# Building the expert router's row lists with a small matrix product instead of a scatter through memory

## The chip, the cores and the metric

The kernel runs on one core of a Trainium2 chip, as one launch. The metric is the device time of that launch in microseconds (us), the median of several executions. All arithmetic is float32.

## What is computed

The reference is a trunk of two layers (`DEPTH = 2`) over 512 latent tokens and 256 context tokens of width 1024. Each layer has a mixer part (a gated long convolution beside latent attention), which the change does not touch, and then a mixture of experts. The first layer handles all 768 tokens, the second only the 512 latent ones. The part that matters here:

```python
def hier_moe(u, w_rg, b_rg, w_re, b_re, w_gate, w_up, w_down):
    t = u.reshape(-1, D_MODEL)
    lg = (t @ w_rg)
    g_sel = jnp.argmax(lg + b_rg, axis=-1)                      # 1 of 8 groups
    p_g = take(softmax(lg), g_sel)
    le_g = (t @ w_re).reshape(T, 8, 8)[g_sel]; be_g = b_re[g_sel]
    _, local = lax.top_k(le_g + be_g, 2)                        # 2 of 8 experts in it
    w_local = softmax(take(le_g, local))
    expert = g_sel * 8 + local; weight = p_g * w_local
    # each expert e: y += weight * ((silu(x @ w_gate[e]) * (x @ w_up[e])) @ w_down[e])
```

There are 64 experts (`NE`), each with 3 MB of weights. Every token picks two of them.

## The kernel before

The program is a sequence of stages. `stage` (line 110 on) opens buffers and semaphores, runs one instruction list per engine, and ends with a barrier over all engines, so nothing of one stage starts before everything of the one before has ended, except transfers that were started early on purpose.

For each layer `experts` (line 2113 on) runs these stages:

1. `norm_stage` normalises the residual. While it runs, `first_round` on the SP queue starts to load the weights of the first four experts into a ring of four places (`RU = 4`; buffers `wgu`, 64 KB per partition, and `wd`, 32 KB per partition).
2. `router_stage` (line 1540 on). For each tile of 128 tokens (`NT` = 6 in the first layer, 4 in the second) TensorE transposes the tokens to rows and computes the 72 router scores (lines 1611 and 1616). The rows are written to the DRAM tensor `rows_in`, twice, once for each of the two picks (line 1583). VectorE then finds the group and the two experts of each token in a chain of small instructions, each waiting for the last (`Chain`, line 120). The result is a one-hot array `sel` (line 1699). Three products on TensorE (lines 1621 to 1623) count for each pick how many earlier picks went to the same expert: `rank`, and the totals `cnt`. `rank_done` announces them.
   After that VectorE computes for each pick the place `dest` in a table: the expert's column and the position in it, or, for an expert with more than 64 picks, a column of an overflow block (lines 1719 to 1742). GpSimd sends each pick's row number to that place in the DRAM tensor `slots` with one indirect DMA per tile and pick, 12 in the first layer and 8 in the second (line 1597). SP waits for all of them, loads the table back into `m.table` (line 1585) and ends the stage.
3. `moe_stage` (line 1788 on) goes through the 64 experts. For expert j GpSimd gathers up to 64 token rows from `rows_in` by the table's column j (line 1834, after a clearing `memset`, line 1830, for each of the first four), TensorE transposes them (1777), multiplies with gate and up weights (`gate_up`, 1761), ScalarE and VectorE form `h` (1911, 1928), TensorE multiplies with the down weights (`down_both`, 1769), and GpSimd scatters the result to `rows_out` by the same column (1841). SP loads expert j's weights when expert j-4's down product is done (lines 1784 and 1785), so the fifth expert's weights start only when the first expert has gone all the way through. The first four and the last four experts are unrolled, those between are a loop (`rounds`).
4. `overflow_stage` handles experts with more than 64 picks, `combine_stage` adds the weighted results to the residual.

The order of the work around the change is thus set by the barriers, by VectorE's chain, and in the experts' stage by the ring of four weights. The lines that decide when the next weights may be fetched:

```python
            def load(j, b, r):
                if inner(j) or j >= RU:
                    wait(sp, s["down_done"], j - (RU - 1))
                    load_expert(sp, a, l, j, wgu[:, b], wd[:, b], loaded[b])
```

Of the kernel before, what the change touches and what calls it, by code (L numbers as in the profile page):

```python
# [69 lines left out]
def layout_constants():  # L70
# [34 lines left out]
    iota = np.zeros((P, 96), f)  # L105
    iota[:, 0:64] = np.arange(64)
    iota[:, 64:88] = np.arange(24)
    iota[:, 88] = np.arange(P)
# [1433 lines left out]
def router_stage(nc, m, l, a, consts, streams, dram):  # L1542

# [6 lines left out]
    NOV = overflow_blocks(n_tok)  # L1550
    NB = NE + NOV
    QM = (n_tok - 1) // SLOTS
    R = NG + NE
    LOW = -3.0e38
    sems = ["consts_in", "wr_in", "bias_in", "tr_done", "lg_done", "tr_evac_a", "tr_evac_v", "lg_evac", "u_out0", "u_out1", "dve",
            "exps", "hot_done", "rank_done", "filled", "fill_out", "dest_done", "sc_out", "table_in"]
    bufs = [("wr", [P, KC, R]), ("bias", [P, R]), ("lg", [P, NT, R]), ("utok", [P, 2, D]), ("triu", [P, P]), ("iota", [P, 96]),
            ("gb", [P, NT, NG]), ("c", [P, NT, NG]), ("hot_g", [P, NT, NG]), ("e", [P, NT, NG]), ("leg", [P, NT, EG]),
            ("beg", [P, NT, EG]), ("val", [P, NT, EG]), ("hot1", [P, NT, EG]), ("hot2", [P, NT, EG]), ("big", [P, NT, NE]),
            ("sel", [P, 2, NT, NE]), ("both", [P, NT, NE]), ("before", [P, NT + 1, NE]), ("rank", [P, NT, NE]), ("cnt", [P, NE]), ("ovf", [P, NE]),  # L1560
            ("incl", [P, NE]), ("base", [P, NE]), ("one", [P, NE]), ("r", [P, 16, NT]), ("ex", [P, 2, NT]),
            ("q", [P, 2, NT]), ("pos", [P, 2, NT]), ("eid", [P, 2, NT]), ("ob", [P, 2, NT]), ("z", [P, 2, NT]), ("dest", [P, 2, NT]),
            ("dest_i", [P, 2, NT], I32), ("num", [P, 2, NT]), ("num_i", [P, 2, NT], I32), ("fill", [SLOTS, NB], I32),
            ("cmp", [P, NOV, NE]), ("oe", [P, NOV])]
    table = dram["table"][l]
    with stage(nc, f"route{l}", sems, bufs) as (block, s):
# [3 lines left out]
        def _(sp):  # L1570
# [5 lines left out]
            sp.dma_start(s["iota"][:], consts["iota"]).then_inc(s["consts_in"], 16)  # L1576
# [24 lines left out]

        @block.tensor
        def _(pe):
# [35 lines left out]
        def _(dve):  # L1639
            link = Chain(dve, s["dve"])  # L1640
            nc.vector.memset(s["before"][:, 0], 0.0)
            for j in range(NT):
                dve.wait_ge(s["tr_done"], j + 1)
                if j >= 2:
                    dve.wait_ge(u_out[j % 2], 32 * (j // 2))
# [13 lines left out]
            iota8 = over(s["iota"][:, None, 0:NG], NT, NG)  # L1659
# [25 lines left out]
            big4 = s["big"][:].rearrange("p t (g j) -> p t g j", g=NG)  # L1685
            for src, dst in ((s["lg"][:, :, NG:R].rearrange("p t (g j) -> p t g j", g=NG), s["leg"]),
                             (over(s["bias"][:, NG:R].rearrange("p (t g j) -> p t g j", t=1, g=NG), NT, NG, EG), s["beg"])):
                link(nc.vector.tensor_tensor(big4, src, hot_over, ALU.mult))
                link(nc.vector.tensor_reduce(dst[:], s["big"][:].rearrange("p t (g j) -> p t j g", g=NG), axis=AX.X, op=ALU.add))
# [4 lines left out]
            picked(s["ex"][:, 0], s["leg"][:], s["hot1"][:])  # L1694
            picked(s["ex"][:, 1], s["leg"][:], s["hot2"][:])
            link(nc.vector.tensor_tensor(row(6), s["ex"][:, 0], s["ex"][:, 1], ALU.max))
            nc.vector.tensor_tensor(s["ex"][:], s["ex"][:], over(row(6)[:, None, :], 2, NT), ALU.subtract).then_inc(s["exps"], 1)
            for k, hot in enumerate((s["hot1"], s["hot2"])):
                last = nc.vector.tensor_tensor(s["sel"][:, k].rearrange("p t (g j) -> p t g j", g=NG), hot_over,
                                               over(hot[:, :, None, :], NT, NG, EG), ALU.mult)  # L1700
            link(last)
            link(nc.vector.tensor_tensor(s["both"][:], s["sel"][:, 0], s["sel"][:, 1], ALU.add))
# [7 lines left out]

            dve.wait_ge(s["exps"], 4)
# [5 lines left out]

            dve.wait_ge(s["rank_done"], 1)
            nc.vector.tensor_copy(s["rank"][:], m.ps[:, 6, 0:NT * NE].rearrange("p (t e) -> p t e", e=NE))
            nc.vector.memset(s["one"][:], 1.0)  # L1720
            link(nc.vector.tensor_copy(s["cnt"][:], m.ps[:, 7, 0:NE]))
            link(nc.vector.tensor_scalar(s["ovf"][:], s["cnt"][:], float(SLOTS), None, ALU.is_gt))
            for q in range(2, QM + 1):
                link(nc.vector.scalar_tensor_tensor(s["ovf"][:], s["cnt"][:], float(q * SLOTS), s["ovf"][:], ALU.is_gt, ALU.add))
            link(nc.vector.tensor_tensor_scan(s["incl"][:], s["one"][:], s["ovf"][:], 0.0, ALU.mult, ALU.add))
            link(nc.vector.tensor_tensor(s["base"][:], s["incl"][:], s["ovf"][:], ALU.subtract))
            for k in range(2):
                for vals, out in ((s["rank"][:], s["pos"]), (over(s["iota"][:, None, 0:NE], NT, NE), s["eid"]), (over(s["base"][:, None, :], NT, NE), s["ob"])):
                    link(nc.vector.tensor_tensor(s["big"][:], s["sel"][:, k], vals, ALU.mult))
# [58 lines left out]
def moe_stage(nc, m, l, a, dram, ring):  # L1788
# [6 lines left out]
    with stage(nc, f"moe{l}", sems, bufs) as (block, s):  # L1795
# [384 lines left out]
```

## Time and profile before

| | us |
|---|---|
| median of 3 runs | 3326.81 (3319.71 to 3334.4) |
| profiled execution | 3327.05 |
| its span, first to last instruction | 3325.3 |
| PE busy | 2768.1 (83%) |
| DVE busy | 869.4 (26%) |
| ACT busy | 630.3 (19%) |
| POOL busy | 372.7 (11%) |

The engines are PE (TensorE; PEld is its weight load), DVE (VectorE), ACT (ScalarE), POOL (GpSimd) and SP (SyncE, which issues most transfers). "Busy" adds up the times of an engine's instructions. The span and the time of the same execution differ by 1.75 us. The mixers and the two expert parts follow each other, so a share of the whole span is a mean over stages that have different limits.

### The profile page before, as it was taken

What the parts mean: (1) busy time and instruction counts of PE and PEld (TensorE: products, weight loads), DVE (VectorE), ACT (ScalarE), POOL (GpSimd) and SP (SyncE); (2) the same over time, 40 slices, a digit from 0 to 9 for tenths busy, and PEclk for the clock granted to TensorE, in tenths of its full rate; (3) what the DMA queues carried; (4) which work ended last, traced back from release to release, by engine and by line L of the source; (5) the groups of instructions that cost most, each with busy time, mean ns of one, the idle gap of its engine ahead of it and who ended that gap; (6) DMA issues with size and microseconds to landing.
All of it is one profiled execution on the core that took longest, in us unless ns stands there. A gap on an engine that the chain in (4) does not pass through costs nothing. (4 is left out here: it accounts for less than half of the span.)

```text
span 3325.3 us, 36651 instructions
## 1 busy us (share of the span) xinstructions
PE 2768.1 (83%) x13443; PEld 1707.5 (51%) x13443; DVE 869.4 (26%) x1741; ACT 630.3 (19%) x1210; POOL 372.7 (11%) x444
## 2 busy tenths in 40 slices
PE   6998987999999982888888578799999749888884
PEld 3445656556655562555555355556544435555553
DVE  3442247144200014111111233424300131111113
ACT  2332210133200010211111121023200111111111
POOL 0000001000000001222222100100000022222221
PEclk7877998999999985999999779999999779999995
DMA  9553111001013032899999521201022429999982
GB/s 334 212 190 139 64 49 65 4 11 43 19 38 107 0 152 83 318 407 393 382 393 382 224 79 48 73 6 48 0 76 88 170 102 408 385 394 383 396 343 78
DMA packets 207096, 589.02 MB, mean 177 GB/s; under 512 B 48336, under 2 KB 105475, under 8 KB 156708
## 3 DMA queue, kind: packets, MB, share of 16 engines
q1 hardware_dynamic: 183428, 556.40, 43.9%
q0 software_dynamic: 23584, 31.53, 2.8%
q8 instruction: 49, 0.80, 0.1%
q14 instruction: 35, 0.29, 0.0%
HBM read 577.29 MB, written 56.68 MB: 191 GB/s over the span
## 5 line engine op out<-in xcount | busy, mean ns | idle before, releaser
L1761 PE MATMUL ps<-wgu,moe_xt 128*64 128x256 f32 x4096 | 509.1, 404 | 147.1 <-DMA wd<-in_w_down_e 144.6
L1761 PEld LDWEIGHTS ps<-wgu,moe_xt 128*64 128x64 f32 x4096 | 336.3, 145 | 277.9 <-issue 168.6
L1356 PE MATMUL ps<-u,w_merge 128*128 128x512 f32 (+1 forms) x768 | 282.3, 526 | 4.1 <-DVEq L1373 4.1
L1769 PE MATMUL ps<-wd,moe_ht 128*64 128x512 f32 x1024 | 247.8, 605 | 1.5 <-DVE moe_ht L1934 1.5
L720 PE MATMUL ps<-u,w_hy 128*128 128x512 f32 (+1 forms) x576 | 213.8, 530 | 18.4 <-PEq L123 18.4
L1928 DVE TENSOR_TENSOR moe_h<-ps,moe_sg 64x256 f32<-64x256 f32 x128 | 54.5, 426 | 664.0 <-ACT moe_sg L1911 664.0
L1356 PEld LDWEIGHTS ps<-u,w_merge 128*128 128x128 f32 x768 | 147.0, 192 | 135.0 <-issue 123.9
L1841 POOL DMA_INDIRECT rows_out<-moe_y,table x128 | 118.5, 926 | 800.7 <-DVE moe_y L1892 788.6
L1777 PE MATMUL ps<-ident,moe_xg 64*128 64x64 f32 x1024 | 140.2, 278 | 74.2 <-DMA moe_xg<-rows_in,table 74.2
L1777 PEld LDWEIGHTS ps<-ident,moe_xg 64*128 64x128 f32 x1024 | 122.7, 199 | 123.0 <-issue 123.0
L720 PEld LDWEIGHTS ps<-u,w_hy 128*128 128x128 f32 x576 | 109.9, 194 | 113.7 <-issue 109.2
L1911 ACT ACTIVATE moe_sg<-ps 64x256 f32<-64x256 f32 x128 | 48.0, 375 | 618.8 <-PE ps L1761 618.8
L1892 DVE COPY moe_y<-ps 64x512 f32<-64x512 f32 x128 | 88.7, 693 | 265.9 <-PE ps L1769 265.9
L1414 PE MATMUL ps<-mix,w_out 128*128 128x512 f32 (+1 forms) x384 | 141.0, 530 | 7.7 <-PEq L123 7.7
L1380 DVE TENSOR_TENSOR merge_t<-ps,merge_sig 128x1024 f32<-128x1024 f32 (+1 forms) x24 | 25.1, 1047 | 397.5 <-ACT merge_sig L1368 397.5
L1834 POOL DMA_INDIRECT moe_xg<-rows_in,table x128 | 120.0, 937 | 42.9 <-issue 36.6
L1414 PEld LDWEIGHTS ps<-mix,w_out 128*128 128x128 f32 x384 | 74.1, 194 | 74.6 <-issue 71.4
L1898 ACT ACTIVATE moe_y<-ps 64x512 f32<-64x512 f32 x128 | 75.6, 590 | 173.4 <-PE ps L1769 173.4
L1898 ACT ACTIVATE moe_xt<-ps 128x512 f32<-128x512 f32 x128 | 76.5, 598 | 166.5 <-PE ps L1777 166.5
L1769 PEld LDWEIGHTS ps<-wd,moe_ht 128*64 128x64 f32 x1024 | 62.3, 136 | 83.5 <-issue 73.1
L1187 PE MATMUL ps<-vt,attn_pt 128*128 x832 | 101.6, 271 | 0.6 <-DVE attn_pt L1288 0.5
L1187 PEld LDWEIGHTS ps<-vt,attn_pt 128*128 128x128 f32 x832 | 98.8, 192 | 1.1 <-ACT attn_pt L1246 1.1
(295 smaller groups left out, 3318.9 us busy)
## 6 DMA issues: line engine op xcount, KB each, us to landing
wgu<-in_w_gate_e SPq DMA_DIRECT2D x128, 1024.0 KB, 8.4
wgu<-in_w_up_e SPq DMA_DIRECT2D x128, 1024.0 KB, 11.0
wd<-in_w_down_e SPq DMA_DIRECT2D x128, 1024.0 KB, 17.2
prep_w<-in_w_ada SPq DMA_DIRECT2D x24, 2048.0 KB, 14.7
w_merge<-in_w_in SPq DMA_DIRECT2D x32, 512.0 KB, 4.7
w_hy<-in_w_in SPq DMA_DIRECT2D x6, 2048.0 KB, 8.4
transfer<-prep_out POOLq DMA_DIRECT2D x10, 1024.0 KB, 7.6
rows_in<-route_utok SPq DMA_DIRECT2D x20, 512.0 KB, 3.6
```

The source lines that it names most:

```text
L720: last = nc.tensor.matmul(m.ps[:, 2 * (i % 2) + t, 0:n], w[:, (i // HC) % 2, c, (i % HC) * P:(i % HC + 1) * P], m.u[:, c, at:at + n], star ...
L1187: last = nc.tensor.matmul(m.ps[:, 6 + u % 2, 0:VD], s["pt"][:, u % 2, k], m.vt[:, k0 // P + k, bass.ds((i * 2 + h) * VD, VD)], start=k == ...
L1356: last = nc.tensor.matmul(m.ps[:, bank, 0:n], w[:, b, w_at + c], z[:, c, at:at + n], start=c == 0, stop=c == kn - 1)
L1414: last = nc.tensor.matmul(m.ps[:, 2 * (k % 2) + t, 0:n], w[:, k // 4, c, (k % 4) * P:(k % 4 + 1) * P], m.mix[:, c, at:at + n], start=c == ...
L1761: last = nc.tensor.matmul(ps[k * SLOTS:(k + 1) * SLOTS, 0:DE], xt[:, c], wgu[:, k, c], start=c == 0, stop=c == KC - 1)
L1769: last = nc.tensor.matmul(ps[k * SLOTS:(k + 1) * SLOTS, 0:512], ht[:, c], wd[:, c, k * 512:(k + 1) * 512], start=c == 0, stop=c == 1)
L1777: last = nc.tensor.transpose(ps[:, c * SLOTS:(c + 1) * SLOTS], src.rearrange("p (q c) -> p c q", c=n)[:, c], ident[0:SLOTS, 0:SLOTS])
L1834: nc.gpsimd.indirect_dma_start(out=xg[:, j % 4], out_offset=None, in_=dram["u"], in_offset=bass.IndirectOffsetOnAxis(ap=m.table[0:SLOTS, j ...
L1841: nc.gpsimd.indirect_dma_start(out=dram["y"], out_offset=bass.IndirectOffsetOnAxis(ap=m.table[0:SLOTS, j:j + 1], axis=0), in_=y[:, j % 2], ...
L1892: copy(y[:, b % 2, half * 512:(half + 1) * 512], m.ps[half * SLOTS:(half + 1) * SLOTS, 5 + b % 2]).then_inc(sem, 1)
L1898: return nc.scalar.activation(out, in_, ACT.Copy)
L1928: nc.vector.tensor_tensor(h[:, b % 2], m.ps[SLOTS:2 * SLOTS, b % 2, 0:DE], sg[SLOTS:2 * SLOTS, b % 2], ALU.mult).then_inc(s["h_done"], 1)
```

## The change

The table is no longer sent through DRAM. In the router stage two one-hot arrays are made: `slot`, which marks for each pick its position among the 64 of its expert, and `tag`, which is `sel` times the pick's row number minus 1536. The product of the two over all picks, 12 (8) accumulating matrix products on TensorE, is the table, negative where a slot is filled and 0 where it is empty. VectorE adds 1536 and has `table` for the scatter. A second array `rows` folds both picks of a token to one row number, so that `rows_in` holds each token once and is written once. The weights of the picks are computed later in VectorE's chain than before.

The columns for overflow blocks, and the list of the experts they belong to, are made in the experts' stage: `late_slots` at the start of VectorE's list there, before its first `h`; a product on TensorE after the fourth expert; `late_lists` on VectorE after that. To hand `sel`, `pos`, `cnt` and `iota` over, they are kept in buffers of `experts`. `rows` is allocated ahead of the ring of weights.

```diff
+            iota[:, 88 + k * TT + j] = k * TOK + j * P + np.arange(P) - 2 * TOK
...
-def router_stage(nc, m, l, a, consts, streams, dram):
+def router_stage(nc, m, l, a, consts, streams, dram, picks):
...
-            sp.wait_ge(s["filled"], 1)
-            sp.dma_start(table.rearrange("(s b) o -> s (b o)", b=NB), s["fill"][:]).then_inc(s["fill_out"], 16)
             for j in range(NT):
...
-                for k in range(2):
-                    sp.dma_start(dram["u"][k * TOK + j * P:k * TOK + (j + 1) * P], s["utok"][:, j % 2]).then_inc(u_out[j % 2], 16)
-            sp.wait_ge(s["sc_out"], 16 * 2 * NT)
-            sp.dma_start(m.table[0:SLOTS, 0:NB], table.rearrange("(s b) o -> s (b o)", b=NB)).then_inc(s["table_in"], 16)
+                sp.dma_start(dram["u"][j * P:(j + 1) * P], s["utok"][:, j % 2]).then_inc(u_out[j % 2], 16)
             for k in range(2):
-                sp.wait_ge(u_out[k], 16 * NT)
-            sp.wait_ge(s["table_in"], 16)
-
-        @block.gpsimd
-        def _(pool):
-            nc.gpsimd.memset(s["fill"][:], NO_ROW).then_inc(s["filled"], 1)
-            pool.wait_ge(s["fill_out"], 16)
-            pool.wait_ge(s["dest_done"], 2)
-            for k in range(2):
-                for j in range(NT):
-                    nc.gpsimd.indirect_dma_start(out=table, out_offset=bass.IndirectOffsetOnAxis(ap=s["dest_i"][:, k, j:j + 1], axis=0),
-                                                 in_=s["num_i"][:, k, j:j + 1], in_offset=None,
-                                                 bounds_check=SLOTS * NB - 1, oob_is_err=False).then_inc(s["sc_out"], 16)
-            pool.wait_ge(s["sc_out"], 16 * 2 * NT)
+                sp.wait_ge(u_out[k], 16 * (NT // 2))
...
             last.then_inc(s["rank_done"], 1)
+            pe.wait_ge(s["slots_done"], 1)
+            for k in range(2):
+                for j in range(NT):
+                    last = nc.tensor.matmul(m.ps[0:SLOTS, 0, 0:NE], s["slot"][:, k, j], s["tag"][:, k, j],
+                                            start=k == 0 and j == 0, stop=k == 1 and j == NT - 1)
+            last.then_inc(s["table_done"], 1)
...
-            dve.wait_ge(s["exps"], 2)
-            link(nc.vector.tensor_reduce(row(2), s["e"][:], axis=AX.X, op=ALU.add))
-            picked(row(3), s["e"][:], s["hot_g"][:])
...
-            picked(s["ex"][:, 0], s["leg"][:], s["hot1"][:])
-            picked(s["ex"][:, 1], s["leg"][:], s["hot2"][:])
-            link(nc.vector.tensor_tensor(row(6), s["ex"][:, 0], s["ex"][:, 1], ALU.max))
-            nc.vector.tensor_tensor(s["ex"][:], s["ex"][:], over(row(6)[:, None, :], 2, NT), ALU.subtract).then_inc(s["exps"], 1)
...
             last.then_inc(s["hot_done"], 1)
 
+            rows = iota[:, 88:88 + 2 * TT].rearrange("p (k t) -> p k t", k=2)[:, :, 0:NT]
+            for k in range(2):
+                nc.vector.tensor_tensor(s["tag"][:, k], sel[:, k, 0:NT], over(rows[:, k, :, None], NT, NE), ALU.mult)
+            dve.wait_ge(s["exps"], 2)
+            link(nc.vector.tensor_reduce(row(2), s["e"][:], axis=AX.X, op=ALU.add))
+            picked(row(3), s["e"][:], s["hot_g"][:])
+
+            dve.wait_ge(s["rank_done"], 1)
+            link(nc.vector.tensor_copy(s["rank"][:], m.ps[:, 6, 0:NT * NE].rearrange("p (t e) -> p t e", e=NE)))
+            for k in range(2):
+                last = nc.vector.tensor_tensor(s["big"][:, k], sel[:, k, 0:NT], s["rank"][:], ALU.mult)
+            link(last)
+            link(nc.vector.tensor_reduce(pos[:, :, 0:NT], s["big"][:], axis=AX.X, op=ALU.add))
+            for k in range(2):
+                last = nc.vector.tensor_tensor(s["slot"][:, k], over(iota[:, None, 0:SLOTS], NT, SLOTS), over(pos[:, k, 0:NT, None], NT, SLOTS), ALU.is_equal)
+            last.then_inc(s["slots_done"], 1)
+            nc.vector.tensor_copy(cnt[:], m.ps[:, 7, 0:NE])
+            picked(s["ex"][:, 0], s["leg"][:], s["hot1"][:])
+            picked(s["ex"][:, 1], s["leg"][:], s["hot2"][:])
...
+            dve.wait_ge(s["table_done"], 1)
+            listed = m.ps[0:SLOTS, 0, 0:NE]
+            link(nc.vector.tensor_scalar(s["late"][:], listed, -float(TOK), -float(TOK), ALU.is_ge, ALU.mult))
+            nc.vector.scalar_tensor_tensor(m.rows[0:SLOTS, 0:NE], listed, float(NO_ROW), s["late"][:], ALU.add, ALU.add)
+            nc.vector.tensor_scalar_add(m.table[0:SLOTS, 0:NE], listed, float(NO_ROW))
...
@@ moe_stage
-                                             in_offset=bass.IndirectOffsetOnAxis(ap=m.table[0:SLOTS, j:j + 1], axis=0),
+                                             in_offset=bass.IndirectOffsetOnAxis(ap=m.rows[0:SLOTS, j:j + 1], axis=0),
...
+            def late_lists():
+                pe.wait_ge(s["late_slots"], 1)
+                for k in range(2):
+                    for j in range(NT):
+                        last = nc.tensor.matmul(m.ps[0:SLOTS, 7, 0:NOV], s["slot"][:, k, j], s["tag"][:, k, j],
+                                                start=k == 0 and j == 0, stop=k == 1 and j == NT - 1)
+                last.then_inc(s["late_table"], 1)
+
             x_transposes(0, 0, 0)
-            rounds(pe, body)
+            rounds(pe, body, late_lists)
...
+            late_slots()
+            rounds(dve, body, late_lists)
...
@@ experts
-    with ExitStack() as whole:
+    with nc.sbuf_tensor(f"rows{l}", [P, NE + overflow_blocks(TOK)], I32) as rows, ExitStack() as whole:
+        m.rows = rows
```

How the instructions move on VectorE, in the first layer's router stage, from the copy of the ranks on. Before, every row from here to the cast of `route_num_i` stands ahead of the first indirect scatter (the second pick repeats rows L1729 and L1730):

```order
L1719 COPY route_rank<-ps 128x384
L1720 MEMSET route_one 128x64
L1721 COPY route_cnt<-ps 128x64
L1722 TENSOR_SCALAR route_ovf<-route_cnt 128x64
L1724 SCALAR_TENSOR_TENSOR route_ovf<-route_cnt,route_ovf 128x64 x10
L1725 SCALAR_TENSOR_TENSOR route_incl<-route_one,route_ovf 128x64
L1726 TENSOR_TENSOR route_base<-route_incl,route_ovf 128x64
L1729 TENSOR_TENSOR route_big<-route_sel,route_rank 128x384
L1730 TENSOR_REDUCE route_pos<-route_big 128x6
...
L1734 SCALAR_TENSOR_TENSOR route_q<-route_pos,route_q 128x12 x10
```

Now (line numbers of the changed program), from the totals before it on; `route_slot` is the array that the table's product waits for:

```order
L1682 TENSOR_TENSOR route_before<-route_before,route_both 128x64 x5
L1689 TENSOR_TENSOR route_tag<-pick_sel,pick_iota 128x384 x2
L1691 TENSOR_REDUCE route_r<-route_e 128x6
L1654 TENSOR_TENSOR route_c<-route_e,route_hot_g 128x48
L1655 TENSOR_REDUCE route_r<-route_c 128x6
L1695 COPY route_rank<-ps 128x384
L1697 TENSOR_TENSOR route_big<-pick_sel,route_rank 128x384 x2
L1699 TENSOR_REDUCE pick_pos<-route_big 128x12
L1701 TENSOR_TENSOR route_slot<-pick_iota,pick_pos 128x384 x2
L1703 COPY pick_cnt<-ps 128x64
```

Four instruction groups (L1695 to L1701) are left between the ranks and the product; the overflow arithmetic has gone from here.

It stands now at the start of VectorE's list in the experts' stage, ahead of the first `moe_h` (some rows of the piece; the order before had `moe_h` as the stage's first row):

```order
L1923 MEMSET moe_one 128x64
L1924 TENSOR_SCALAR moe_ovf<-pick_cnt 128x64
...
L1930 TENSOR_TENSOR moe_big<-pick_sel,moe_base 128x384 x2
L1932 TENSOR_REDUCE moe_ob<-moe_big 128x12
...
L1943 TENSOR_TENSOR moe_slot<-pick_iota,moe_at 128x384
L1944 TENSOR_TENSOR moe_tag<-pick_iota,moe_ob 128x144
...
L1949 TENSOR_TENSOR moe_cmp<-moe_incl,pick_iota 128x1536
L1951 TENSOR_REDUCE moe_oe<-moe_cmp 128x24
L1952 TENSOR_SCALAR moe_oe<-moe_oe 128x24
L1953 CAST over<-moe_oe 128x24
L1954 CAST over<-moe_incl 128x1
L1909 TENSOR_TENSOR moe_h<-ps,moe_sg 64x256
```

The whole piece is 28 instructions in either layer, all but a few linked one to the next.

## Rows read from the trace of the kernel before

**Rows 1.** The page: the costliest group, and one of its transfers by its issues
```profile
L1761 PE MATMUL ps<-wgu,moe_xt 128*64 128x256 f32 x4096 | 509.1, 404 | 147.1 <-DMA wd<-in_w_down_e 144.6
...
wd<-in_w_down_e SPq DMA_DIRECT2D x128, 1024.0 KB, 17.2
```

**Rows 2.** Windows: stretch, its us, busy of each engine, clock, DMA share, GB/s
```profile
1346.00:1400.00 54.00, 50.28 (x354) 29.54 (x352) 9.98 (x22) 11.06 (x22) 13.03 (x14) 0.97 0.99 387
1500.00:1860.00 360.00, 305.81 (x2081) 186.16 (x2082) 58.65 (x125) 64.47 (x124) 77.31 (x83) 0.95 0.99 386
```

**Rows 3.** Timeline, layer 0, ranks to first h: start, us, engine, line, [idle before]
```profile
1288.74 0.56 DVE L1719 COPY route_rank<-ps 128x384 f32<-128x384 f32 x1 [2.50 <-PE ps L1623]
...
1325.68 0.94 POOL L1830 MEMSET moe_xg<- 64x1024 f32 x1 [4.18 <-POOLq L123]
1327.45 0.99 POOL L1834 DMA_INDIRECT moe_xg<-rows_in,table  x1 [0.83 <-POOL moe_xg L1830]
...
1338.09 0.43 DVE L1928 TENSOR_TENSOR moe_h<-ps,moe_sg 64x256 f32<-64x256 f32 x1 [29.09 <-ACT moe_sg L1911]
```

**Rows 4.** Timeline, layer 1: the same three moments
```profile
2681.08 0.42 DVE L1719 COPY route_rank<-ps 128x256 f32<-128x256 f32 x1 [1.67 <-PE ps L1623]
...
2708.71 0.94 POOL L1830 MEMSET moe_xg<- 64x1024 f32 x1 [4.49 <-POOLq L123]
...
2720.68 0.43 DVE L1928 TENSOR_TENSOR moe_h<-ps,moe_sg 64x256 f32<-64x256 f32 x1 [24.61 <-ACT moe_sg L1911]
```

**Rows 5.** Timeline, layer 0: row writes, and pieces of VectorE's chain that move or remain
```profile
1254.62 17.17 SPq L1583 DMA_DIRECT2D rows_in<-route_utok  x12
...
1274.41 0.20 DVE L1681 TENSOR_REDUCE route_r<-route_e 128x6 f32<-128x48 f32 x1 [0.31 <-ACT route_e L1634]
...
1275.13 0.56 DVE L1688 TENSOR_TENSOR route_big<-route_lg,route_hot_g 128x384 f32<-128x384 f32 x1
...
1280.95 0.21 DVE L1671 TENSOR_TENSOR route_c<-route_leg,route_hot 128x48 f32<-128x48 f32 x1
...
1282.20 1.02 DVE L1699 TENSOR_TENSOR route_sel<-route_hot_g,route_hot 128x384 f32<-128x384 f32 x2
...
1293.48 0.55 DVE L1730 TENSOR_REDUCE route_pos<-route_big 128x6 f32<-128x384 f32 x1
```

**Rows 6.** Timeline: TensorE after idling, a router product and a 64-wide weight load
```profile
1253.57 3.53 PE L1616 MATMUL ps<-route_wr,u 128*128 128x72 f32 x16
...
1332.81 0.26 PEld L1761 LDWEIGHTS ps<-wgu,moe_xt 128*64 128x64 f32 x2 [0.16 <-issue]
```

**Rows 7.** Timeline, GpSimd: the first instruction after the barrier into the router stage
```profile
1248.25 0.16 POOL L1592 MEMSET route_fill<- 64x88 int32 x1 [0.74 <-POOLq L123]
```

**Rows 8.** Timeline: VectorE and GpSimd beside each other, layer 0, then layer 1
```profile
1304.68 1.75 DVE L1749 TENSOR_TENSOR route_cmp<-route_incl,route_iota 128x1536 f32<-128x1536 f32 x1
1305.71 1.70 POOL L1597 DMA_INDIRECT slots<-route_num_i,route_dest_i  x1 [57.30 <-DVE route_num_i L1747]
...
1307.71 1.01 POOL L1597 DMA_INDIRECT slots<-route_num_i,route_dest_i  x1 [0.30 <-issue]
1308.25 0.47 DVE L1752 TENSOR_SCALAR route_oe<-route_oe 128x24 f32<-128x24 f32 x1
...
2693.13 1.22 DVE L1749 TENSOR_TENSOR route_cmp<-route_incl,route_iota 128x1024 f32<-128x1024 f32 x1
2694.10 1.17 POOL L1597 DMA_INDIRECT slots<-route_num_i,route_dest_i  x1 [51.54 <-DVE route_num_i L1747]
```

**Rows 9.** Windows of the program's start, columns as in rows 2
```profile
10.00:15.00 5.00, 0.33 (x2) 0.18 (x1) 0.00 (x0) 1.99 (x5) 0.00 (x0) 1.00 1.00 406
35.00:40.00 5.00, 5.00 (x24) 1.22 (x24) 2.93 (x4) 0.00 (x0) 0.00 (x0) 0.50 1.05 410
45.00:50.00 5.00, 4.13 (x20) 1.22 (x24) 1.10 (x2) 0.82 (x2) 0.00 (x0) 0.66 1.06 393
50.00:55.00 5.00, 4.23 (x40) 2.34 (x32) 3.57 (x5) 2.11 (x5) 0.00 (x0) 1.00 1.10 350
```

More of the change, by code:

```diff
@@ L1657, in row @@
                 return s["r"][:, k]
-            iota8 = over(s["iota"][:, None, 0:NG], NT, NG)
+            iota8 = over(iota[:, None, 0:NG], NT, NG)
             def first_max(val, hot, k):
@@ L1716, in _ @@
             nc.vector.tensor_tensor(m.weight[:, :, 0:NT], s["ex"][:], over(row(8)[:, None, :], 2, NT), ALU.mult)
[L1718 to L1729, printed above, removed]
-                    link(nc.vector.tensor_reduce(out[:, k], s["big"][:], axis=AX.X, op=ALU.add))
@@ L1731, in _ @@
-            link(nc.vector.tensor_scalar(s["q"][:], s["pos"][:], float(SLOTS), None, ALU.is_ge))
-            link(nc.vector.tensor_copy(s["z"][:], s["q"][:]))
-            for q in range(2, QM + 1):
-                link(nc.vector.scalar_tensor_tensor(s["q"][:], s["pos"][:], float(q * SLOTS), s["q"][:], ALU.is_ge, ALU.add))
-            link(nc.vector.scalar_tensor_tensor(s["ob"][:], s["ob"][:], float(NE - 1), s["q"][:], ALU.add, ALU.add))
-            link(nc.vector.tensor_tensor(s["ob"][:], s["ob"][:], s["eid"][:], ALU.subtract))
@@ L1743, in _ @@
-            for k in range(2):
-                for j in range(NT):
-                    last = nc.vector.tensor_scalar_add(s["num"][:, k, j:j + 1], s["iota"][:, 88:89], float(k * TOK + j * P))
-            link(last)
-            nc.vector.tensor_copy(s["num_i"][:], s["num"][:]).then_inc(s["dest_done"], 1)
-            link(nc.vector.tensor_tensor(s["cmp"][:], over(s["incl"][:, None, :], NOV, NE),
-                                         over(s["iota"][:, 64:64 + NOV][:, :, None], NOV, NE), ALU.is_le))
@@ L1751, in _ @@
-            link(nc.vector.tensor_reduce(s["oe"][:], s["cmp"][:], axis=AX.X, op=ALU.add))
-            link(nc.vector.tensor_scalar(s["oe"][:], s["oe"][:], float(NE - 1), None, ALU.min))
-            nc.vector.tensor_copy(m.over[:, 1:1 + NOV], s["oe"][:])
-            nc.vector.tensor_copy(m.over[:, 0:1], s["incl"][:, NE - 1:NE])
 def gate_up(nc, ps, xt, wgu):
@@ new lines, in late_lists @@
+            def late_lists():
+                link = Chain(dve, s["dve"], LATE_LINKS)
+                listed = m.ps[0:SLOTS, 7, 0:NOV]
+                dve.wait_ge(s["late_table"], 1)
+                link(nc.vector.tensor_scalar(s["late"][:], listed, -float(TOK), -float(TOK), ALU.is_ge, ALU.mult))
+                nc.vector.scalar_tensor_tensor(m.rows[0:SLOTS, NE:NE + NOV], listed, float(NO_ROW), s["late"][:], ALU.add, ALU.add)
+                nc.vector.tensor_scalar_add(m.table[0:SLOTS, NE:NE + NOV], listed, float(NO_ROW))
@@ L2015, in body @@
                 dve.wait_ge(s["block_done"], i + 1)
+                nc.vector.tensor_scalar(s["row"][:], m.rows[0:SLOTS, bass.ds(i + NE, 1)], 0.0, None, ALU.add)
                 nc.vector.tensor_scalar(s["idx"][:], m.table[0:SLOTS, bass.ds(i + NE, 1)], 0.0, None, ALU.add).then_inc(s["idx_done"], 1)
@@ L2124, in first_round @@
                 load_expert(sp, a, l, b, wgu[:, b], wd[:, b], ring[2][b])
+        picks = {name: whole.enter_context(nc.sbuf_tensor(f"pick_{name}{l}", shape, F32))
+                 for name, shape in (("sel", [P, 2, TT, NE]), ("pos", [P, 2, TT]), ("cnt", [P, NE]), ("iota", [P, IOTA_COLS]))}
         with nc.sbuf_tensor(f"u2_{l}", [P, KC, TOK], F32) as u:
@@ L2139, in trunk @@
         m = chip_memory(nc, ctx)
-        dram = {"u": nc.dram_tensor("rows_in", [A_ALL, D], F32).ap(), "y": nc.dram_tensor("rows_out", [A_ALL, D], F32).ap(),
-                "table": [nc.dram_tensor(f"slots{l}", [SLOTS * (NE + overflow_blocks(TOK if l < DEPTH - 1 else SEQ)), 1],
-                                         I32).ap() for l in range(DEPTH)],
+        dram = {"u": nc.dram_tensor("rows_in", [TOK, D], F32).ap(), "y": nc.dram_tensor("rows_out", [A_ALL, D], F32).ap(),
                 "h": [[nc.dram_tensor(f"transfer{l}_{t}", [2, P, 2, (SEQ, CTX)[t] // P // 2, 2, HW], F32).ap() for t in range(2)]
```

114 lines of the change are left out of this document (76 added, 38 removed).

## The prediction

> **What bounds the kernel now.** I began with the page: its costliest group is the experts' gate and up product, and TensorE's idle time before it, 147.1 us in all, ended with the landing of expert weights [rows 1]. The windows say why: inside the experts' stages the transfer engines are 0.99 busy at 386 to 387 GB/s [rows 2]. There are 128 experts in the two layers, with three transfers of 1024 KB each [rows 1]; 120 of them are loaded inside the stages (the ring holds the first 4 of each layer), so 120 x 3.146 MB at 387 GB/s is 975 us in which memory sets the pace. Since the fifth expert's load waits for the first expert's down product, this stream starts when the first expert is through, and its end moves with its start. Before that start nothing covers the router: in layer 0 the ranks reach VectorE at 1288.74, the stage after the router begins at 1325.68 with GpSimd's memset, the first gather is issued at 1327.45 and the first `h` is made at 1338.09 [rows 3]. In layer 1 the same runs from 2681.08 over 2708.71 to 2720.68 [rows 4]. So the time from ranks to the next stage, 36.9 and 27.6 us, is on the path in full, and I read the change there.
>
> **What goes.** All of that time is replaced: VectorE's table arithmetic, 12 and 8 scatters, the wait for them, and the load of the table. With it go two waits ahead of the ranks. The sum of the exponentials and its two followers stood between 1274.10 (0.31 before the first of them) and 1275.13, 1.0 us; the six instructions on `ex` stood from 1280.95 to 1282.20, 1.25 us [rows 5]. Both now run behind the ranks' products or the table's, so the ranks come 2.25 us earlier in layer 0; for the narrower layer 1 I estimate 2.1. The two new `tag` products beside them (a pair of this size takes 1.02 [rows 5]) and the three instructions of the first block come to about 1.9 us and fit into the 2.50 us that VectorE idles before the ranks in layer 0 [rows 3], where by moving the five weight instructions away there is another microsecond.
>
> **What comes in its place, layer 0.** The rank copy 0.56 [rows 3] and a link, 0.6; a pair of products 1.05 and a pair of comparisons 1.05, by the pair's row; one reduction over 768 elements, which I put at 1.0 from 0.55 for half of it [rows 5]. That is 3.7 us. Then 12 accumulating products on TensorE, which has idled. No row has this shape. From above: after such an idle stretch 8 products of 72 columns with 128-wide weights take 3.53, 0.44 each; from below: two 64-wide weight loads in a slow stretch take 0.26 [rows 6]. I take 0.35, between them, because the weights here are the narrow ones and the moving operand is short: 4.2, and 0.15 to start. VectorE then makes the two lists and the five weight instructions, 8 small ones at about 0.2: 1.6. The barrier: GpSimd idled 0.74 between stages [rows 7], I take 0.85. Together 10.5, against 36.9: 26.4 gained, with the 2.25 it is 28.7.
>
> **Layer 1**, with 256 columns for 384: 2.8 + 8 x 0.35 + 0.15 + 1.5 + 0.85 = 8.1, against 27.6: 19.5, with 2.1 it is 21.6. Both layers: 50.3.
>
> **What comes behind the barrier.** VectorE's 28 instructions of `late_slots` stand ahead of the first `h`. From the same rows, with 1.75 and 1.22 for the comparison of `incl` [rows 8] and as much for its reduction, they add up to 11.3 us in layer 0 and 9.0 in layer 1. The first `h` came 12.4 and 12.0 us after the memset [rows 3, 4]. Run alone they are just hidden, by 1.1 and 3.0 us; without the cover they would cost all of it. But GpSimd clears and gathers beside them. The trace has this meeting once per layer: a scatter that began under a comparison took 1.70 and not 1.01, and ended at 1307.41, 0.98 after the comparison's end at 1306.43; in layer 1 it took 1.17 and ended 0.92 after 2694.35. A small VectorE instruction that began inside a scatter took 0.47 and ended with it, at 1308.72 [rows 8]. So I let either side wait for the other: the first gather meets the pair on `big` and loses at most 0.7, and VectorE's list is longer by what it waits. I charge 1.4 in layer 0, where the margin is thin, and 0.5 in layer 1. The ends: nothing, and 4 gathers and 4 memsets at about 0.97 each added whole to the list, which makes it 19.0 and 16.8 and the first `h` late by 6.6 and 4.8, 11.4 in all.
> The Trainium skill (SBUF — State Buffer, Who interferes with whom) infers that a tensor_tensor does not hold up descriptor generation, and says beside it that a VectorE instruction with two SBUF inputs contends with a GpSimd one that reads SBUF. By the inference alone the gathers would lose nothing and the sum would be 0.7 us better; rows 8 side with the second statement.
>
> **What costs nothing.** The 20 products for overflow lists after the fourth expert: the weight stream has begun three experts earlier and is 0.99 busy from 1346 on [rows 2], TensorE being ahead of it; without that cover they cost 20 x 0.27, 5.4. Halved writes of `rows_in`: the last was issued by 1271.8 [rows 5], long before the ranks. The gathers read the same number of rows.
>
> **The sum.** 50.3 - 1.9 = 48.4; 3327.05 - 48.4 = 3278.7, so **3279 us**. The profiled execution and the median of the runs (3326.81) are 0.24 apart, so no correction. Bounds: products at 0.26 give -1.8, at 0.44 give +1.8; the opening -1.9 to +9.5; the late products up to +5.4; the runs shown spread by 7 us to either side. From below 3279 - 1.8 - 1.9 - 7, above 3279 + 1.8 + 9.5 + 5.4: **3268 to 3296**.
>
> **Rivals.** 0.5% is 16.6 us, about what a measurement of this kernel can tell from no change.
> *A, the late list is the new bound.* VectorE is still in `late_slots` when the first silu is ready, and everything shifts. For it: a margin of 1.1 us and rows 8. Against it: most of the instructions are under 0.25 us and leave gaps. Price: half to all of 11.4, less the 1.9 charged: 3283 to 3289. Chance 0.2.
> *B, the weight stream gets a little slower.* `rows`, 88 integers or 352 bytes, now lies ahead of `wgu`, so every weight row lands 96 bytes off a multiple of 256 where it lay on one. The token and table loads at the program's start had starts off by 32 in the built program; the stretch with the tokens ran at 406 GB/s, the later one at 393, against 410 for aligned weights [rows 9]. 1% to 4.3% of 975 us: 10 to 42 us, 3289 to 3321. Against it: 406 is as good as any, and the 393 has shorter rows in it. Chance 0.04.
> The Trainium skill (DMA: Bandwidth & Descriptors, How a descriptor splits into AXI transactions) gives the vendor's account, by which a row of 8 KB off such a boundary takes 33 pieces for 32; an estimate from that is 3.1%, 30 us, 3309. No run here shows it.
> *C, slower than before,* by the same place: from 6.6% slower loads, (3343.4 - 3279) / 975, the kernel is slower by over 0.5%, from 4.9% the gain is gone. The worst stretch of such loads had 350 GB/s against 410 [rows 9], 17%: 3279 + 166 = 3445. Against it: that stretch carries rows of 1 KB and less, the weights' are 8 KB. Chance 0.02.
> *D, the list isn't what the stage waits for.* If the writes of `rows_in` or the table's users ended the router stage, the gain would be less than half, 3303 or more. The last write was issued 17 us before the ranks [rows 5], so 0.01.
>
> **How the numbers follow.** Forecast 0.73, A 0.2, B 0.04, C 0.02, D 0.01. The range takes in A, the bounds and the spread, and leaves B's upper part, C and D out, and what runs add. Faster by over 0.5% means under 3310.2: forecast, A, half of B, D: 0.95; within: 0.03; slower: 0.02.
>
> **What would show it.** Right: no GpSimd scatter to `slots`; from the rank copy to GpSimd's first memset 10 to 11 us in layer 0 and about 8 in layer 1; 12 and 8 products of 3 to 5 and 2 to 3.5 us there; the first `h` 12 to 14 us after the memset; windows of the experts' stages still at 386 or more. Wrong: an `h` whose idle time ends with VectorE's own list (A), or windows under 380 GB/s (B, C).

## The result, and the profile after

The changed kernel took 3285.44 us (3274.44 to 3287.16) against 3327.24 us before; the ratio is 0.9874 with a 95% interval of 0.9855 to 0.9894. It is 41.8 us faster where 48 were forecast, inside the range of 3268 to 3296. The profiled executions are 39.9 us apart in their spans, 3325.3 and 3285.4.

The page of the changed kernel; the group answers to rows 1:

```profile
span 3285.4 us, 36721 instructions
...
PE 2780.2 (85%) x13523; PEld 1727.6 (53%) x13523; DVE 869.2 (26%) x1709; ACT 630.3 (19%) x1210; POOL 355.6 (11%) x422
...
L1727 PE MATMUL ps<-wgu,moe_xt 128*64 128x256 f32 x4096 | 512.6, 406 | 154.5 <-DMA wd<-in_w_down_e 152.3
```

VectorE is as busy as before, 869.2 us for 869.4: what the change takes from it in one place it adds in another. What shrank is the time in which nothing else could run. Its timeline in layer 0, from the rank copy to the fifth expert's first weight load (columns as in rows 3):

```profile
1284.84 0.56 DVE L1695 COPY route_rank<-ps 128x384 f32<-128x384 f32 x1 [1.94 <-PE ps L1600]
...
1288.57 2.82 PE L1605 MATMUL ps<-route_tag,route_slot 128*64 128x64 f32 x24 [3.83 <-DVE route_slot L1701]
...
1292.76 0.17 DVE L1720 TENSOR_TENSOR weight<-route_ex,route_r 128x12 f32<-128x12 f32 x1
1293.68 0.94 POOL L1803 MEMSET moe_xg<- 64x1024 f32 x1 [47.76 <-POOLq L125]
...
1293.79 0.88 DVE L1924 TENSOR_SCALAR moe_ovf<-pick_cnt 128x64 f32<-128x64 f32 x1
1294.71 0.20 DVE L1925 TENSOR_SCALAR moe_ovf<-moe_ovf 128x64 f32<-128x64 f32 x1
...
1302.67 1.75 DVE L1949 TENSOR_TENSOR moe_cmp<-moe_incl,pick_iota 128x1536 f32<-128x1536 f32 x1
...
1303.84 1.40 POOL L1807 DMA_INDIRECT moe_xg<-rows_in,rows  x1 [0.77 <-POOL moe_xg L1803]
...
1305.63 0.38 ACT L1892 ACTIVATE moe_sg<-ps 64x256 f32<-64x256 f32 x1 [3.93 <-PE ps L1727]
...
1306.70 0.43 DVE L1909 TENSOR_TENSOR moe_h<-ps,moe_sg 64x256 f32<-64x256 f32 x1
...
1314.38 0.35 SPq L1750 DMA_DIRECT2D wgu<-in_w_gate_e  x1
```

From the rank copy to the memset it is 8.84 us where it was 36.94 [rows 3]. In layer 1:

```profile
2654.99 0.42 DVE L1695 COPY route_rank<-ps 128x256 f32<-128x256 f32 x1 [1.40 <-PE ps L1600]
...
2657.78 1.97 PE L1605 MATMUL ps<-route_tag,route_slot 128*64 128x64 f32 x16 [2.90 <-DVE route_slot L1701]
...
2662.02 0.94 POOL L1803 MEMSET moe_xg<- 64x1024 f32 x1 [42.12 <-POOLq L125]
...
2674.49 0.42 DVE L1909 TENSOR_TENSOR moe_h<-ps,moe_sg 64x256 f32<-64x256 f32 x1 [1.54 <-ACT moe_sg L1892]
...
2682.62 0.35 SPq L1750 DMA_DIRECT2D wgu<-in_w_gate_e  x1
```

Here it is 7.03 us for 27.63 [rows 4]. Together 48.7 us went, and the reordering ahead of the ranks gave 2.30 and 2.14 more (from the start of the first reduction on `gb` to the rank copy 16.28 and 13.32 us before, 13.98 and 11.18 after). That is 53.1, more than the 39.9 by which the span shrank. Something gave some 13 us back.

It is the weight stream. In the kernel before, layer 0, it begins with the first row below, the fifth expert's first load; at the second row the last expert's gate and up product starts:

```profile
1346.22 0.35 SPq L1784 DMA_DIRECT2D wgu<-in_w_gate_e  x1
...
1864.52 0.86 PE L1761 MATMUL ps<-wgu,moe_xt 128*64 128x256 f32 x5 [0.83 <-DMA wd<-in_w_down_e]
```

and in the changed kernel that product starts here:

```profile
1839.08 3.67 PE L1727 MATMUL ps<-wgu,moe_xt 128*64 128x256 f32 x32 [0.98 <-DMA wd<-in_w_down_e]
```

For the same 60 experts that is 518.3 us before and 524.7 after (1839.08 - 1314.38). In layer 1, 3237.80 - 2728.80 = 509.0 before and 3198.16 - 2682.62 = 515.5 after. I call these two lengths the stretches from here on. They grew by 12.9 us. The windows from the middle of the stages agree (columns as in rows 2), first of before:

```profile
1400.00:1800.00 400.00, 339.26 (x2352) 207.82 (x2350) 67.19 (x143) 73.91 (x142) 87.55 (x94) 0.97 1.00 393
2800.00:3180.00 380.00, 322.13 (x2232) 195.98 (x2228) 62.52 (x133) 69.74 (x134) 82.90 (x89) 0.96 0.99 390
```

then of the changed kernel:

```profile
1370.00:1770.00 400.00, 334.38 (x2327) 213.16 (x2325) 64.92 (x138) 71.86 (x138) 88.65 (x94) 0.97 1.01 388
2760.00:3140.00 380.00, 321.21 (x2208) 196.29 (x2206) 63.08 (x134) 69.33 (x133) 83.92 (x89) 0.96 0.99 383
```

The transfer engines are as fully busy and move 1.3 and 1.8% less.

### The profile page after: what moved, and what is told of

Read it like the earlier page. It is cut to its first block and busy times, and to the rows that moved or that the text cites. A ratio compares the mean times of both kernels' runs of the same rounds, so it can differ in the third digit from the quotient of the medians.

```text
span 3285.4 us, 36721 instructions
## 1 busy us (share of the span) xinstructions
PE 2780.2 (85%) x13523; PEld 1727.6 (53%) x13523; DVE 869.2 (26%) x1709; ACT 630.3 (19%) x1210; POOL 355.6 (11%) x422
## 5 line engine op out<-in xcount | busy, mean ns | idle before, releaser
L1727 PEld LDWEIGHTS ps<-wgu,moe_xt 128*64 128x64 f32 x4096 | 350.5, 146 | 274.5 <-issue 172.1
L1807 POOL DMA_INDIRECT moe_xg<-rows_in,rows x128 | 122.9, 960 | 43.0 <-issue 36.6
L1018 PE MATMUL ps<-u,w_qkv 128*128 128x512 f32 (+1 forms) x272 | 93.8, 506 | 4.3 <-PEq L125 4.3
```

The lines of the kernel that those rows point to most:

```text
L1018: last = nc.tensor.matmul(m.ps[:, 2 * (i % 2) + t, 0:n], lhs, m.u[:, c, at:at + n], start=c == 0, stop=c == KC - 1)
L1727: last = nc.tensor.matmul(ps[k * SLOTS:(k + 1) * SLOTS, 0:DE], xt[:, c], wgu[:, k, c], start=c == 0, stop=c == KC - 1)
L1807: nc.gpsimd.indirect_dma_start(out=xg[:, j % 4], out_offset=None, in_=dram["u"], in_offset=bass.IndirectOffsetOnAxis(ap=m.rows[0:SLOTS, j: ...
```

## The experiments

**Is it where the weights land?** Theory 1 is rival B of the prediction: `rows` pushed the ring off a multiple of 256 bytes. Four kernels on one chip, beside 11 runs of the kernel before (3327.46 us). In the built programs the ring starts at a multiple of 256 bytes before the change and 96 bytes past one after it.

The changed kernel as it is:

> The changed kernel as it is, beside the others on one chip, as the base line for them. Every theory: about 42 us faster than before, near 3285 us; the fifth expert's first weight load about 32 us (layer 0) earlier than before; from that load to the last gate and up product 6 us longer per layer than before (518.3 before, 524.7 after in layer 0; 509.0 and 515.5 in layer 1).

3289.14 us, ratio 0.9886 (0.9861 to 0.9911); stretches 526.7 and 515.0.

The same with the ring back on a multiple of 256:

```diff
-    with nc.sbuf_tensor(f"rows{l}", [P, NE + overflow_blocks(TOK)], I32) as rows, ExitStack() as whole:
+    with nc.sbuf_tensor(f"rows{l}", [P, 128], I32) as rows, ExitStack() as whole:
```

> The changed kernel with rows widened from 88 to 128 integers, 512 bytes, so that the ring of weights begins on a multiple of 256 bytes again, as before the change. Theory 1 (the weight stream lost 1.3% because its rows land 96 bytes off such a multiple): the stretch from the fifth expert's load to the last gate and up product goes back to 518 and 509 us, the kernel to about 3272 us, 13 us faster than the changed one. Theory 2 (the stream is slower for another reason that the change brought: the DRAM addresses, the gathers' pattern, an earlier start): the stretches stay at 525 and 515 us and the time at 3285. Theory 3 (the difference between the two profiled executions is scatter): neither differs from the other beyond the spread.

3268.70 us, ratio 0.9842 (0.9817 to 0.9866), 58.8 us faster than before and 20.4 faster than the changed kernel beside it. The stretches are 519.5 and 510.6, and its windows are near the old rates (393 and 390 GB/s before, 388 and 383 in the changed kernel):

```profile
1355.00:1755.00 400.00, 336.74 (x2351) 216.04 (x2347) 66.31 (x141) 73.33 (x141) 88.97 (x94) 0.97 1.00 393
2740.00:3120.00 380.00, 325.27 (x2230) 196.67 (x2232) 63.52 (x135) 70.41 (x135) 83.30 (x88) 0.96 0.99 387
```

This is the version that beats both kernels. The 20.4 is a difference of medians; by the two ratios it is 14.6 us. Its stretches account for 11.6. Its profiled execution was also 12.0 us ahead of that of the changed kernel when it issued its first expert load (1199.6 for 1211.6), before any buffer that the edit moves is used, so scatter can make the rest.

On a multiple of 128 but not of 256:

```diff
-    with nc.sbuf_tensor(f"rows{l}", [P, NE + overflow_blocks(TOK)], I32) as rows, ExitStack() as whole:
+    with nc.sbuf_tensor(f"rows{l}", [P, 96], I32) as rows, ExitStack() as whole:
```

> The changed kernel with rows widened to 96 integers, 384 bytes: the ring begins 128 bytes past a multiple of 256, but on a multiple of 64. Theory 1a (every start off a multiple of 256 costs one more piece per row of 8 KB, whichever offset): like the changed kernel, 3285 us and 525 and 515 us. Theory 1b (only the odd 32 bytes cost): like the ring on 256, 3272 us. Theory 2: 3285.

3288.89 us, ratio 0.9878 (0.9853 to 0.9903), like the changed kernel; stretches 527.0 and 516.0. Variant 1b, the odd 32 bytes, falls.

The kernel before, only shifted:

```diff
-    with ExitStack() as whole:
+    with nc.sbuf_tensor(f"shift{l}", [P, 88], I32) as shift, ExitStack() as whole:
```

> The kernel before with an unused buffer of 352 bytes ahead of the ring, nothing else changed: only the alignment of the weights' destination differs. Theory 1: 13 us slower than before, near 3340 us, with the stretches at 525 and 515 us in place of 518 and 509. Theories 2 and 3: no difference from before, 3327 us.

3347.88 us (3337.83 to 3353.98), ratio 1.0062 (1.0039 to 1.0086): 20.4 us slower, by the interval 13 to 29, where 13 were expected. The stretches are 524.9 and 515.3, 12.9 together, as expected, and the rates are near those of the changed kernel:

```profile
1400.00:1800.00 400.00, 332.36 (x2342) 206.08 (x2342) 65.34 (x139) 72.35 (x139) 86.93 (x94) 0.98 1.00 389
2810.00:3190.00 380.00, 318.77 (x2219) 195.76 (x2221) 62.09 (x132) 68.86 (x132) 84.07 (x90) 0.97 0.99 385
```

Nothing differs from the kernel before but the addresses of the ring and of the buffers allocated behind it, so theories 2 (DRAM layout, gathers, earlier start) and 3 (scatter) fall. Of the 20.4 us, the 7.5 outside the stretches are not explained.

**Does the offset's size, or the share of rows that are off, set the price?** Three variants of the kernel before, each run once. An unused buffer of 32 bytes ahead of the ring (`before_off_32`); 96 bytes between `wgu` and `wd` (`only_wd_off`); 96 ahead of `wgu` and 160 between the two (`only_wgu_off`):

```diff
-    with ExitStack() as whole:
+    with nc.sbuf_tensor(f"shift{l}", [P, 8], I32) as shift, ExitStack() as whole:
... only_wd_off
         wgu = whole.enter_context(nc.sbuf_tensor(f"wgu{l}", [P, RU, 2, KC, DE], F32))
+        whole.enter_context(nc.sbuf_tensor(f"shift{l}", [P, 24], F32))
... only_wgu_off
+        whole.enter_context(nc.sbuf_tensor(f"shift{l}", [P, 24], F32))
         wgu = whole.enter_context(nc.sbuf_tensor(f"wgu{l}", [P, RU, 2, KC, DE], F32))
+        whole.enter_context(nc.sbuf_tensor(f"back{l}", [P, 40], F32))
```

> The kernel before with an unused buffer of 32 bytes ahead of the ring. Theory 1a (any start off a multiple of 256 costs the same): the two stretches from the fifth expert's load to the last gate and up product are 525 and 515 us, like those with an offset of 96 or 128. Theory 1c (the cost grows with the bytes past the boundary): about 520 and 511, a third of it.

> The kernel before with 96 unused bytes between wgu and wd: the gate and up weights (two thirds of the bytes) land on multiples of 256 as before, the down weights 96 bytes past one. Theory 1a (the cost lies in the landing of each off row): a third of the 6.3 us per layer, stretches near 520.5 and 511 us against 518.3 and 509.0 of the kernel before and 525 and 515 with all rows off. If it lay in TensorE's reading of the gate and up weights instead: no change, 518 and 509.

> The kernel before with 96 unused bytes ahead of wgu and 160 between wgu and wd: the gate and up weights land 96 bytes off, the down weights on multiples of 256. Theory 1a: two thirds, near 522.5 and 513 us.

All stretches together, each from one profiled execution. The last four rows are the changed kernel again and the three variants of it that follow below, all with the ring 96 bytes off. The last two columns are the mean time of one transfer packet of 8 KB inside the stretches, layer 0 and layer 1, from the same traces:

```
run              offset of wgu, wd   layer 0   layer 1   sum over before   packet, ns
before                 0,  0          518.3     509.0        0            329.6  327.3
ring_on_256            0,  0          519.5     510.6        2.8          330.3  327.9
only_wd_off            0, 96          518.5     512.7        3.9          330.5  330.5
only_wgu_off          96,  0          521.4     512.2        6.3          332.5  331.1
before_shifted        96, 96          524.9     515.3       12.9          334.6  331.1
before_off_32         32, 32          527.0     516.3       16.0          335.2  333.6
changed kernel        96, 96          524.7     515.5       12.9          334.8  331.1
ring_on_128          128,128          527.0     516.0       15.7          334.7  332.0
same_after            96, 96          526.7     515.0       14.4          335.1  331.9
product_x6            96, 96          527.9     516.2       16.8          335.5  331.6
late_twice            96, 96          525.9     516.8       15.4          334.9  331.9
no_late               96, 96          528.5     516.3       17.5          336.6  332.6
```

Eight executions with every row off cost 12.9 to 17.5 us, the two with none off 0 and 2.8. 32, 96 and 128 bytes cost about the same, so variant 1c (a price by the bytes past the boundary) falls. With a third of the bytes off it was 3.9, with two thirds 6.3, against 4.2 and 8.4 expected. That is in the right order, but a single value is uncertain by 3 to 5 us, as the rows with equal offsets show, so the 3.9 alone can't be told from nothing.

What decides between the landing of the rows and TensorE's reading of them is the packets. With all rows off they took 1.5 to 2.1% longer in layer 0 and 1.2 to 1.9% in layer 1 than in the kernel before, and less or as much where some were. One matrix instruction of the gate and up product took 404 and 406 ns on the two aligned kernels and 402 to 410 on the eight with all rows off, with no order in it. So it is the transfer that got slower. The times were 3353.12 us (3327.51 before, on its chip), 3327.75 and 3335.05 (3329.07 before, on theirs).

**Is the rest of the router's end on the path in full?** The table's product six times over:

```diff
+            for again in range(6):
-            for k in range(2):
-                for j in range(NT):
+                for k in range(2):
+                    for j in range(NT):
```

> The changed kernel with the table's product computed six times over (72 and 48 matrix products where 12 and 8 stood, same result). Theory 1 (from the ranks to the experts' stage everything is on the path in full): at 0.235 us a product, as the changed kernel's trace has them at the lower clock, 14.1 and 9.8 us more, 24 in all, about 3311 us; if the granted clock rises during the longer product, less per product, down to 14 us in all. The stretch from the rank copy to GpSimd's first memset grows by the same amount in either layer, the weight streams stay at 525 and 515 us. Theory 2 (the stage's end waits for something else, the row writes or the barrier, within some us): clearly less than the product's growth appears in the stage and in the time.

3308.28 us (3300.62 to 3308.97), ratio 0.9935 (0.9923 to 0.9948), 16 us over the changed kernel's ratio of 0.9886 and 20 over its 0.9874. From rank copy to memset it is 15.98 and 13.38 us, 7.14 and 6.35 more, just what TensorE's product grew by (9.97 us for 2.82, and 8.32 for 1.97); the fifth expert's first load comes 7.7 and 7.3 us later after the ranks, 15 in all. Theory 1 holds; that it was nearer to 14 than to 24 is the clock's doing:

```profile
L1606 PEld LDWEIGHTS ps<-route_tag,route_slot x240: 138/138/232, 1282.9 to 2670.8; 128*64 128x64 f32 x120
L1606 PE MATMUL ps<-route_tag,route_slot x240: 222/222/369, 1282.9 to 2670.9; 128*64 128x64 f32 x120
```

(columns: minimum, median and maximum in ns of one matrix instruction; a product of the kernel is two). In layer 0 the granted clock was 0.50 up to 1284.50 and 1.00 from 1286.50 to the end, and the median instruction took 222 ns, for 314 in the changed kernel. There, in the short product, the clock stayed at 0.50, the lower of its two levels, 1.2 GHz:

```profile
1288.50:1291.40 2.90, 2.82 (x24) 2.64 (x24) 1.21 (x8) 0.21 (x1) 0.00 (x0) 0.50 0.00 0
```

**How near is VectorE's list to being the bound?** The arithmetic ahead of the first `h` twice:

```diff
-            late_slots()
+            late_slots(False)
+            late_slots(True)
             rounds(dve, body, late_lists)
```

(`False` leaves the signal to the late product away, so that only the second copy gives it.)

> The changed kernel with the overflow arithmetic ahead of the first h done twice (the first copy's result is overwritten by the same values). Theory A (VectorE's list ahead of the first h has used up its cover, so each further us is paid): the first h moves from 13.0 to about 24.5 us after the memset in layer 0 and from 12.5 to about 20 in layer 1, 19 us in all, about 3306 us. Rival (the weight ring or the product path hides it further): less than 5 us in the time.

3310.16 us (3296.53 to 3312.60), ratio 0.9942 (0.9928 to 0.9956), 19 us over the changed kernel's ratio of 0.9886 and 23 over its 0.9874. The first `h` came 23.99 and 19.61 us after the memset, 11.0 and 7.1 later than in the changed kernel. In layer 0:

```profile
1279.26 0.94 POOL L1803 MEMSET moe_xg<- 64x1024 f32 x1 [47.82 <-POOLq L125]
...
1303.09 0.14 DVE L1958 CAST over<-moe_incl 128x1 int32<-128x1 f32 x1
1303.25 0.43 DVE L1909 TENSOR_TENSOR moe_h<-ps,moe_sg 64x256 f32<-64x256 f32 x1
1303.82 0.47 PE L1743 MATMUL ps<-ident,moe_h 64*128 64x64 f32 x2 [11.59 <-DVE moe_h L1909]
1304.21 6.27 PE L1727 MATMUL ps<-wgu,moe_xt 128*64 128x256 f32 x32
```

TensorE idles 11.59 us for it. The cover is used up: what is added here is paid, and more than once. The fifth expert's first load came 13.6 and 8.3 us later after the memset, not 11.0 and 7.1. While TensorE idled its granted clock fell from 1.00 to 0.50, and the second expert's gate and up product took 6.27 us, where the changed kernel has 3.67 at 1.00. (In layer 1 it idled 7.10 us, and the product took 5.21.)

```profile
1291.00:1294.00 3.00, 1.23 (x10) 0.96 (x8) 2.76 (x11) 0.97 (x2) 0.00 (x0) 1.00 0.11 33
1294.00:1297.00 3.00, 0.00 (x0) 0.00 (x0) 2.73 (x10) 0.00 (x0) 0.00 (x0) 0.81 0.00 0
1297.00:1300.00 3.00, 0.00 (x0) 0.00 (x0) 2.90 (x9) 0.00 (x0) 0.00 (x0) 0.50 0.00 0
1304.20:1308.20 4.00, 4.00 (x21) 2.28 (x22) 0.29 (x1) 0.00 (x0) 0.00 (x0) 0.50 0.00 0
```

And without the overflow lists at all, which leaves out a part of the computation that holds no block in these inputs:

```diff
-            rounds(pe, body, late_lists)
+            rounds(pe, body)
...
                 link = Chain(dve, s["dve"])
-                nc.vector.memset(s["one"][:], 1.0)
...
-                nc.vector.tensor_copy(m.over[:, 0:1], s["incl"][:, NE - 1:NE])
+                link(nc.vector.memset(s["one"][:], 0.0))
+                nc.vector.tensor_copy(m.over[:, 0:1], s["one"][:, 0:1])
...
-            rounds(dve, body, late_lists)
+            rounds(dve, body)
```

> The changed kernel without the overflow lists: no such arithmetic before the first h, no late product, no late lists; the count of overflow blocks is set to 0, which it also was. Theory A at its real size: the first h of layer 0 comes 12.4 us after the memset and not 13.0, layer 1 about the same as before; the fourth gather takes 0.95 and not 1.40 us, the first 0.99 and not 1.04, since no VectorE comparison runs beside them. In the time under 1.5 us, which a single look can't tell from nothing.

3286.48 us in its one run, no difference that can be told. The first `h` of layer 0 comes after 12.33 us, now with VectorE waiting:

```profile
1286.11 0.94 POOL L1803 MEMSET moe_xg<- 64x1024 f32 x1 [47.84 <-POOLq L125]
...
1287.94 1.04 POOL L1807 DMA_INDIRECT moe_xg<-rows_in,rows  x1 [0.88 <-POOL moe_xg L1803]
...
1296.12 0.95 POOL L1807 DMA_INDIRECT moe_xg<-rows_in,rows  x1 [0.77 <-POOL moe_xg L1803]
...
1298.44 0.42 DVE L1909 TENSOR_TENSOR moe_h<-ps,moe_sg 64x256 f32<-64x256 f32 x1 [11.95 <-ACT moe_sg L1892]
```

The fourth gather went from 1.40 to 0.95, as expected. The first did not: it took 1.04 with and without VectorE's work beside it, so that part of my expectation was wrong. In layer 1 the first `h` came after 13.48 us, later than in the changed kernel (12.47), so there the list was not what set it; that moment wanders by up to 1.8 us between executions and layers where VectorE's list is absent (11.9 to 13.7).

## Why the prediction was right, and where it was off

- *The path.* That the router's end is uncovered, and that the stream's end moves with its start, held: `product_x6` and `late_twice` pay what they add.
- *What goes and what replaces it.* Forecast 10.5 and 8.1 us from ranks to memset, measured 8.84 and 7.03: 2.7 us better. 2.2 of it is the step "I take 0.35" for a product. It took 0.235 in layer 0 (2.82 / 12) and 0.246 in layer 1 (1.97 / 8). My end from below, 0.26 for a product's two weight loads, was no end: here the 24 loads followed each other at 0.11 (2.64 / 24), 0.22 for two.
- *The waits ahead of the ranks.* Forecast 2.25 and 2.1, measured 2.30 and 2.14.
- *The opening of the experts' stage.* 1.9 charged. The first `h` came 0.60 and 0.49 us later after the memset, the fifth expert's first load, which is what counts, 0.16 and 0.51 later. In layer 0 rival A began to bite: the silu was ready at 1306.01, VectorE took `h` up at 1306.70. It cost tenths of a microsecond because TensorE would have waited anyway: before, the next gate and up product was held up for ScalarE's `moe_xt` and began 1.87 us after the transposes of its rows (1337.58 to 1339.45); with the late `h` it began 2.09 after them (1305.53 to 1307.62).

```profile
1337.58 1.10 PE L1777 MATMUL ps<-ident,moe_xg 64*128 64x64 f32 x8
...
1339.45 3.67 PE L1761 MATMUL ps<-wgu,moe_xt 128*64 128x256 f32 x32 [0.37 <-ACT moe_xt L1898]
```

- *The late product* took 1.5 us on TensorE in layer 0 and did not show: the stretches were no shorter without it (528.5 and 516.3 in `no_late`, the longest of all).
- *The weight stream.* This is the step that failed. I gave rival B a chance of 0.04 at 10 to 42 us, arguing "406 is as good as any" from a window of the program's start. It happened, at 12.9 us, 1.3%. That window, of 5 us, could not exclude it: 406 against 410 is 1%, the size of the effect. And the effect was decided by the address, which I had read. The 975 us that I took the percentage of were 1027.3 (518.3 + 509.0): the 387 GB/s of the windows also count what GpSimd gathers and scatters, 8.39 of 157.04 MB in one of them, not the weights alone. My sign for B, windows under 380 GB/s, was too coarse to show it: they read 388 and 383.
- *The size of that effect.* The Trainium skill (DMA: Bandwidth & Descriptors, How a descriptor splits into AXI transactions) names the boundary, in words about what a transfer fetches, and the runs bear it out for the side on which the rows land: 32, 96 and 128 bytes off cost alike, and moving the ring by 512 bytes cost nothing that can be told. Its count of pieces, 33 for 32 at any of these offsets, would by estimate make 3.1%, twice what was measured. The way its table counts beats would make 257, 259 and 260 for 256 at 32, 96 and 128 bytes off, by estimate 0.4, 1.2 and 1.6%; measured were 1.6%, 1.3 to 1.7% and 1.5%. So neither count gives the price, and `before_off_32` speaks against the second; what sets it stays open.

The terms with their measured sizes: 48.7 + 4.4 - 0.7 - 12.9 = 39.5, against 39.9 between the spans. The forecast of 48.4 was 4.0 too low on the first three and left the last one out; the two errors partly cancelled in the total. That the time fell into the range was in part luck: its upper part was made for a late `h` and for the late products, neither of which cost what it allowed, and it took in the slower stream, for which its bounds had no term.

## What to carry to other kernels

A stage that ends in a barrier and is followed by a stream paced by memory is worth its whole length: replacing a small table's round trip through DRAM (serial arithmetic, one scatter at a time, a load) by a product of one-hot arrays took it from 37 to 9 us. Work that has to move should go where an engine waits, with its length set against the wait: here the list that I put at 11.3 us took 12.9 beside GpSimd's work, and the silu that it had to be ready for came after 12.3. Past that, what is added is paid with a surcharge, as the idle TensorE lost its clock. And before a small buffer is put ahead of large ones that transfers fill, look at their start addresses: 160 bytes of padding took 11.6 us off the two stretches.

## What the runs showed of the hardware that was not expected

- Transfers of 8 KB rows into on-chip memory that started 32, 96 or 128 bytes past a multiple of 256 made the two transfer-bound stretches 1.3 to 1.7% longer in eight executions (12.9 to 17.5 of 1027.3 us), with the transfer engines as busy (0.99 to 1.01 in the windows). The packets themselves took longer, 335 to 337 ns for 330 in layer 0.
- TensorE's granted clock fell from 1.00 to 0.50 while it idled 11.59 us in `late_twice`, and the gate and up product behind the pause took 6.27 us for 3.67.
- VectorE and GpSimd held each other up one instruction at a time. A `TENSOR_SCALAR` on 64 elements that began under GpSimd's memset took 0.88 and not 0.20 and ended 0.05 after it; a gather that began under a comparison with two inputs ended 0.82 after the comparison. The Trainium skill (SBUF — State Buffer, Who interferes with whom) says that a `tensor_scalar` can contend with GpSimd, in a mode that uses both ports, and that an instruction of VectorE with two SBUF inputs contends with one of GpSimd that reads SBUF; these rows agree. Its inference that a `tensor_tensor` does not hold up descriptor generation is not borne out by gathers that read their row numbers on chip: 1.40 with the comparison, 0.95 without.
